# A two-layer conformer and attention trunk on one core: y gets its own buffer, layer 0's sum is transposed block by block unnormalised, ScalarE seeds the taps

## The reference

```python
# layer 0
a, b, z = split(rmsnorm(x, a_norm) @ a_w_in)             # 2048 x 6144
c  = causal_depthwise_conv(a * sigmoid(b), width 31) + conv_b
y  = silu(layernorm(c) * ln_g + ln_b) * silu(z)
x1 = x + y @ a_w_out                                     # 2048 x 2048
# layer 1
kv = rmsnorm(x1, kv_norm) @ w_kv                         # k, v of 3 groups, 16 heads of 128
q, z2 = split(rmsnorm(x1, b_norm) @ b_w_in)              # q of 3 groups, and a gate
o  = merged softmax attention of the 3 dilation groups, bias by distance
x2 = x1 + (o * silu(z2)) @ b_w_out
out = rmsnorm(x2, final_norm)
```

## Time and profile before

| | us |
|---|---|
| median of 3 runs | 1511.68 (1511.62 to 1514.68) |
| the profiled execution | 1510.1 |
| its span | 1508.3 |
| PE busy | 1462.2 |
| DVE busy | 793.9 |
| ACT busy | 689.1 |
| GpSimd busy | 386.7 |

### The profile page before, as it was taken

How to read it: one execution, slowest core, us unless ns; L and a number is a source line. 1 busy time by engine, 2 the same in 40 slices (tenths; PEclk the granted TensorE clock), 3 DMA queues, 4 the chain that set the end, 5 groups by cost and what they waited for, 6 DMA issues and landing times.

```text
span 1508.3 us, 28300 instructions
## 1 busy us (share of the span) xinstructions
PE 1462.2 (97%) x11478; PEld 1414.1 (94%) x11478; DVE 793.9 (53%) x1190; ACT 689.1 (46%) x989; POOL 386.7 (26%) x168
## 2 busy tenths in 40 slices
PE   6999998979999999999999999999999999999997
PEld 5999998868799999999999999999999999999886
DVE  3899999480274454544444444445454454444332
ACT  5434343464474444444444444444444444444543
POOL 4888887568600000000000000000000000000595
PEclk9999999989999999999999999999999999999999
DMA  9666666345399666656666666665665666653652
GB/s 256 176 193 184 183 195 182 117 134 184 111 275 238 179 176 173 183 161 188 187 170 178 167 179 179 178 186 156 191 178 167 177 176 176 184 159 115 251 195 84
DMA packets 454141, 268.52 MB, mean 178 GB/s; under 512 B 4353, under 2 KB 436481, under 8 KB 453426
## 3 DMA queue, kind: packets, MB, share of 16 engines
q1 hardware_dynamic: 454098, 267.99, 62.1%
q10 hardware_dynamic: 6, 0.02, 0.0%
HBM read 263.71 MB, written 4.29 MB: 178 GB/s over the span
## 4 chain that ended last, share of the span: by engine, by line
issue 76%; POOL 18%; PE 5%; POOLq 0%; DVE 0%; ACT 0%
POOL w_lo L271 18%; PE bank L307 2%; PE bank L308 2%; PE bank L309 2%; POOLq L270 0%; ACT bank L681 0%; DVE y L965 0%; DVE resid L949 0%; PE bank L1109 0%; ACT y L702 0%; PE bank L327 0%; PE bank L326 0%; PE bank L325 0%; PE bank L1111 0%; ACT stat L697 0%
## 5 line engine op out<-in xcount | busy, mean ns | idle before, releaser
L262 ACT ACTIVATE w_hi<-raw 128x1024 fp32r<-128x1024 f32 x480 | 506.6, 1059 | 471.5 <-PE bank L289 386.7
L271 POOL TENSOR_TENSOR w_lo<-raw,w_hi 128x1024 fp32r<-128x1024 f32 x160 | 385.7, 2416 | 1105.1 <-ACT w_hi L262 1105.0
L287 PE MATMUL bank<-act_a,w_hi 128*128 128x256 f32 x2304 | 651.0, 283 | 4.7 <-DVE act_b L869 2.4
L288 PE MATMUL bank<-act_a,w_hi 128*128 128x256 f32 x2304 | 646.4, 281 | 0.0
L289 PE MATMUL bank<-act_a,w_lo 128*128 128x256 f32 x2304 | 643.0, 279 | 0.0
L271 DVE TENSOR_TENSOR w_lo<-raw,w_hi 128x1024 fp32r<-128x1024 f32 x320 | 391.6, 1229 | 476.4 <-ACT w_hi L262 476.4
L287 PEld LDWEIGHTS bank<-act_a,w_hi 128*128 128x128 f32 x2304 | 434.6, 189 | 7.0 <-DVE act_b L869 2.6
L288 PEld LDWEIGHTS bank<-act_a,w_hi 128*128 128x128 f32 x2304 | 438.0, 190 | 0.1
L289 PEld LDWEIGHTS bank<-act_a,w_lo 128*128 128x128 f32 x2304 | 434.7, 189 | 0.0
L287 PE MATMUL bank<-act_b,w_hi 128*128 128x256 f32 x1024 | 288.1, 281 | 0.0
L288 PE MATMUL bank<-act_b,w_hi 128*128 128x256 f32 x1024 | 286.4, 280 | 0.0
(11 more groups left out here) (119 smaller groups left out, 767.2 us busy)
## 6 DMA issues: line engine op xcount, KB each, us to landing
raw<-w_kv_dram SPq DMA_DIRECT2D x96, 1024.0 KB, 6.0
raw<-b_w_in_dram SPq DMA_DIRECT2D x64, 1024.0 KB, 6.6
raw<-a_w_in_dram SPq DMA_DIRECT2D x48, 1024.0 KB, 5.9
raw<-a_w_out_dram SPq DMA_DIRECT2D x16, 1024.0 KB, 5.0
raw<-b_w_out_dram SPq DMA_DIRECT2D x16, 1024.0 KB, 5.1
bias<-bias_dram SPq DMA_DIRECT2D x16, 384.0 KB, 8.1
x_sb<-x_dram SPq DMA_DIRECT2D x2, 1024.0 KB, 7.4
resid_dram<-x_sb SPq DMA_DIRECT2D x1, 2048.0 KB, 7.9
```

The lines of the kernel that those rows point to most:

```text
L262: nc.scalar.activation(w_hi[:, stream.half_slot(half), :], raw[:, slot, part:part + HALF], ACT.Copy).then_inc(hi_done, 1)
L271: eng.tensor_tensor(w_lo[:, stream.half_slot(half), :], raw[:, slot, part:part + HALF], w_hi[:, stream.half_slot(half), :].bitcast(F32), A ...
L287: nc.tensor.matmul(dst[:, 0:S], wide_hi, source[:, kt, 0, :], start=(kt == 0), stop=False)
L288: nc.tensor.matmul(dst[:, 0:S], wide_hi, source[:, kt, 1, :], start=False, stop=False)
```

## The change

- `tap`, `seed_taps`: for channel blocks 2 to 15, ACT writes the two accumulators of taps 0 and 1. They lie in three banks in turn. 28 taps stand between two glus.
- The mean moves to z slab 7, the squares to slab 10, the variance to 10, the root to 12.
- y: swish goes from `conv` to three places in PSUM (`y_stage`), is gated there, and its parts go to `mem_y`, a buffer of its own that shares no memory with what z's products read. Swish and parts are one loop; weight slabs 0, 1, 2 of A_OUT are split at its steps 4, 11, 14.
- A block of x1 is transposed unnormalised during the next block (`turn_x1`), and ACT and DVE make the parts for layer 1 from it (`input_hi`, `input_lo`). Behind A_OUT stands only the last block's; PE goes on with QKV halves 0, a part of 1, and 2 around it.
- 1/rms enters behind the products: rows made by PE from scaled identities (`diag`, `anti`) multiply k and z (`scale_head`, DVE), the scores take it with their scale (`q_scale`), v takes it when its rows are copied (`v_scale`; four copies instead of two). ACT copies v and q only.
- SP stores x1 once it is added. ACT's AB loop is written out. Operand buffers have other addresses: all high parts together, then all low parts.

```diff
-Y_LOOP_SPLITS = {7: (2, (0,)), 14: (2, (1,))}
-LATE_Q_INPUT = {2: range(4, 8), 3: range(8, 12), 4: range(12, KT)}
+RAW_SLOTS, HALF_SLOTS = 5, 5
 U_RING = 4
-PAIR_TAPS = 26
-MEAN_SLAB, SQUARE_SLOT, VAR_SLAB, STD_SLOT = 8, 12, 11, 14
+PAIR_TAPS = 28
+SEEDED_FROM = 2
+ACC_BANKS = (4, 5, 7)
+MEAN_SLAB, SQUARE_SLOT, VAR_SLAB, STD_SLOT = 7, 10, 10, 12
+SPREAD = 8
+Y_LOOP_SLABS = (4, 11, 14)
+PART = KT * S
...
+        def act_a(kt, part):
+            first = part * (PART + SPREAD) + kt * S
+            return mem_a[:, first:first + S]
...
+        def y_in(kt, part):
+            first = part * PART + kt * S
+            return mem_y[:, first:first + S]
+        def y2_in(kt, part):
+            first = 80 + part * PART + kt * S
+            return mem_a[:, first:first + S]
...
+        y_stage = [bank[n][:, 0:S] for n in ACC_BANKS]
...
             for half in (2 * j, 2 * j + 1):
+                project_tiles(pe, stream, turn, half, range(KT // 2), dst, source, source_ready).then_inc(mm_done, 1)
...
+                    nc.tensor.matmul(dst[:, 0:S], wide_hi, source(kt, 1), start=False, stop=False)
+                    mm = nc.tensor.matmul(dst[:, 0:S], wide_lo, source(kt, 0),
...
                 mm.then_inc(mm_done, 1)
+        def turned(kt):
+            return bank[4 + 2 * (kt // RKT % 2) + kt % RKT // 2][:, (kt % 2) * S:(kt % 2 + 1) * S]
+        def acc_of(c, k):
...
-                    sp.wait_ge(x1_turned, TT * KT)
+                    sp.wait_ge(x1_added, TT * CHUNKS)
                     sp.dma_start(resid_dram.ap(), x_sb[:, :, :]).then_inc(resid_stored, 16)
...
+            def seed_taps(c):
+                act.wait_ge(u_ready, c + 1)
+                positive(act, tap_done, taps_before(c - 2))
+                for k in range(2):
+                    acc, tap = acc_of(c, k), param[:, c, k:k + 1]
+                    src = u[:, c % U_RING, k:k + S]
+                    if k == 0:
+                        nc.scalar.activation(acc, src, ACT.Identity, bias=param[:, c, ROW_CONV_B:ROW_CONV_B + 1],
+                                             scale=tap).then_inc(seeded, 1)
+                    else:
+                        nc.scalar.activation(acc, src, ACT.Copy, scale=tap).then_inc(seeded, 1)
+            for n in range(2, 2 * KT):
+                split_hi(act, AB, n // 4, n % 4)
+                if n >= 4 and n % 2 == 0:
+                    c = n // 2 - 2
+                    gate_b(c // 2, c % 2)
+                if n >= 5 + 2 * SEEDED_FROM and n % 2 == 1:
+                    seed_taps((n - 5) // 2)
...
+                if n in (1, 3):
+                    seed_taps(KT - 2 + n // 2)
...
+            for kt in range(KT + 1):
+                if kt < KT:
+                    act.wait_ge(ln_scaled, kt // 4 + 1)
+                    if kt >= 3:
+                        act.wait_ge(y_lo, kt - 2)
+                    nc.scalar.activation(y_stage[kt % 3], conv[:, kt, :], ACT.Silu,
+                                         bias=param[:, kt, ROW_LN_B:ROW_LN_B + 1],
+                                         scale=param[:, kt, ROW_LN_G:ROW_LN_G + 1]).then_inc(swished, 1)
+                if kt > 0:
+                    act.wait_ge(y_ready, kt)
+                    nc.scalar.activation(y_in(kt - 1, 0), y_stage[(kt - 1) % 3], ACT.Copy).then_inc(y_hi, 1)
+                if kt in Y_LOOP_SLABS:
+                    j = Y_LOOP_SLABS.index(kt)
+                    split_hi(act, A_OUT, 0, j)
+                    gate_z(KT - 3 + j)
...
+            def input_hi(c):
+                act.wait_ge(x1_turned, c + 1)
+                for kt in range(RKT * c, RKT * (c + 1)):
+                    nc.scalar.activation(act_a(kt, 0)[:, ::-1], turned(kt), ACT.Copy,
+                                         scale=param[:, kt, ROW_KV_NORM:ROW_KV_NORM + 1]).then_inc(kv_hi, 1)
+                for kt in range(RKT * c, RKT * (c + 1)):
+                    act.wait_ge(kv_lo, 2 * (kt // 2 + 1))
+                    nc.scalar.activation(act_b(kt, 0), turned(kt), ACT.Copy,
+                                         scale=param[:, kt, ROW_B_NORM:ROW_B_NORM + 1]).then_inc(qb_hi, 1)
...
+                if q == 3 and c > 0:
+                    input_hi(c - 1)
             split_hi(act, QKV, 0, 0)
+            split_hi(act, QKV, 0, 1, halves=(0,))
             for t in range(TT):
                 square_rows(CHUNKS - 1, t)
...
+            for t in range(TT):
                 act.wait_ge(x1_summed, t + 1)
                 nc.scalar.activation(std[:, t:t + 1], sq_sum[:, t:t + 1], ACT.Sqrt, bias=eps,
                                      scale=1.0 / D).then_inc(x1_std, 1)
...
             split_hi(act, QKV, 0, 1, halves=(1,))
+            act.wait_ge(v_scale_ready, 1)
...
+                    turned_v = bank[5 + b][:, 0:n * S].rearrange("p (g t d) -> p g t d", g=n, t=TT)
+                    for t in range(TT):
+                        nc.scalar.activation(v_rows[:, g0:g0 + n, t, :], turned_v[:, :, t, :], ACT.Copy,
+                                             scale=v_scale[:, t:t + 1]).then_inc(v_copied, 1)
...
+                before = taps_before(c) + (k if c < SEEDED_FROM else k - 2)
+                if c < SEEDED_FROM and k == 0:
                     dve.wait_ge(u_ready, c + 1)
-                    if c > 0:
-                        dve.wait_ge(tap_done, c * (TAPS + 1))
-                if k >= 2:
-                    dve.wait_ge(tap_done, c * (TAPS + 1) + (k - 1))
+                if c >= SEEDED_FROM:
+                    if k < 2:
+                        return
+                    if k == 2:
+                        dve.wait_ge(seeded, 2 * (c - SEEDED_FROM + 1))
+                if k >= (2 if c < SEEDED_FROM else 4):
+                    dve.wait_ge(tap_done, before - 1)
                 if k == 0:
...
+            for kt in range(KT + 1):
+                if kt < KT:
+                    dve.wait_ge(swished, kt + 1)
+                    dve.wait_ge(gate_ready, kt + 1)
+                    nc.vector.tensor_tensor(y_stage[kt % 3], y_stage[kt % 3], gate[:, kt, :],
+                                            ALU.mult).then_inc(y_ready, 1)
+                if kt > 0:
+                    dve.wait_ge(y_hi, kt)
+                    nc.vector.tensor_tensor(y_in(kt - 1, 1), y_stage[(kt - 1) % 3], y_in(kt - 1, 0).bitcast(F32),
+                                            ALU.subtract).then_inc(y_lo, 1)
...
+            def input_lo(c):
+                for kt in range(RKT * c, RKT * (c + 1)):
+                    dve.wait_ge(kv_hi, 2 * (kt // 2 + 1))
+                    nc.vector.scalar_tensor_tensor(
+                        out=act_a(kt, 1)[:, ::-1], in0=turned(kt), scalar=param[:, kt, ROW_KV_NORM:ROW_KV_NORM + 1],
+                        in1=act_a(kt, 0)[:, ::-1].bitcast(F32), op0=ALU.mult, op1=ALU.subtract).then_inc(kv_lo, 1)
+                for kt in range(RKT * c, RKT * (c + 1)):
+                    dve.wait_ge(qb_hi, 2 * (kt // 2 + 1))
+                    nc.vector.scalar_tensor_tensor(
+                        out=act_b(kt, 1), in0=turned(kt), scalar=param[:, kt, ROW_B_NORM:ROW_B_NORM + 1],
+                        in1=act_b(kt, 0).bitcast(F32), op0=ALU.mult, op1=ALU.subtract).then_inc(qb_lo, 1)
             for c in range(CHUNKS - 1):
                 for t in range(TT):
                     add_layer0(c, t)
+                if c > 0:
+                    input_lo(c - 1)
+            input_lo(CHUNKS - 2)
             split_lo(dve, QKV, 0, 0, lo_dve)
-            add_layer0(CHUNKS - 1, 0)
...
             split_lo(dve, QKV, 0, 1, lo_dve, halves=(0,))
...
+            for t in range(TT):
+                add_layer0(CHUNKS - 1, t)
+            for t in range(TT):
+                sum_squares(t, x1_squared, x1_summed)
+            input_lo(CHUNKS - 1)
+            for t in range(TT):
+                dve.wait_ge(x1_std, t + 1)
+                nc.vector.reciprocal(rstd[:, t:t + 1], std[:, t:t + 1]).then_inc(x1_rstd, 1)
+            dve.wait_ge(x1_rstd, TT)
+            for t in range(TT):
+                nc.vector.tensor_scalar(diag[:, t, :], ident[:, :], rstd[:, t:t + 1], None,
+                                        ALU.mult).then_inc(diag_ready, 1)
+                nc.vector.tensor_scalar(anti[:, t, ::-1], ident[:, :], rstd[:, t:t + 1], None,
+                                        ALU.mult).then_inc(diag_ready, 1)
+            nc.vector.tensor_scalar(q_scale, rstd, SCALE, None, ALU.mult).then_inc(r_rows_copied, 1)
             split_lo(dve, QKV, 0, 1, lo_dve, halves=(1,))
+            dve.wait_ge(r_rows_made, 1)
+            nc.vector.tensor_scalar(r_row[:, :], bank[2][:, 0:S], float(D), None, ALU.mult).then_inc(r_rows_copied, 1)
+            nc.vector.tensor_scalar(rk_row[:, ::-1], bank[2][:, 0:S], float(D), None,
+                                    ALU.mult).then_inc(r_rows_copied, 1)
+            dve.wait_ge(r_rows_made, 2)
+            nc.vector.tensor_scalar(v_scale, bank[3][:, 0:TT], float(D), None, ALU.mult).then_inc(v_scale_ready, 1)
```

(89 more changed lines are left out.)

177 lines of the change are left out of this document (59 added, 118 removed).

## The result

The changed kernel takes 1524.49 us (median of 4 runs, 1522.99 to 1525.56); the kernel before took 1512.87 beside it. Ratio 1.0075, interval 1.0058 to 1.0093: 11.6 us slower where no change was forecast.

What follows compares the result with a forecast made beforehand. TensorE, busy 97% of the span, was taken as the bound. Terms 2.6 − 8.0 − 3.4 − 9.7 + 3.0 + 18.8 − 3.7 + 0.8 − 0.3 summed to +0.1 us, forecasting 1511.8 us, range 1501 to 1518.

Steps and rivals of the forecast that it cites:

- New addresses of the operands: All matmuls: pace unchanged by the new operand addresses, 0; a 0.1% change of pace would be ±1.3 us.
- blocks 1 to 3: Output projection A after its first block: transposes moved inside, +3.0 us, and waits at two block ends, +18.8.
- E to the fifth half: From the end of output projection A to QKV's fifth half-slab: −3.7 us, and +0.8 for lost clock.
- Taps seeded: Conv loop: ScalarE seeds taps 0 and 1; PE waits 3.7 us against 1.1 before, +2.6 (bounds 0, +6).
- Mean, variance, handover of y: z stage into output projection: no wait at mean, −8.0 us, or variance, −3.4; y's own buffer, −9.7.
- The forecast wait of 0.7: First output block: PE waits 0.7 us for the second weight slab, split near 305.1.
- T1 and T2: Ends of output projection A's second and third blocks: crossed ScalarE and DVE queues, 2 × 9.4 = +18.8 us.
- Start of QKV: From output projection A's end to QKV's fifth half: store leaves earlier, −3.7 us (bounds −5 and −1).
- E': End of output projection A in the changed kernel, from which the QKV start times are counted.
- Heads: Attention heads: bank reads pass from ACT to DVE, covered, 0; +7 us if the cover were gone.
- the prediction's rivals: T1/T2 waits absent, 1493 us, 15% (half hidden, 1502, 5%); conv loop behind, 1521, 13%; heads lose cover, 1519, 7%.
- The one that reached furthest up, 1521: Conv loop falls behind at the GLU product of channels 7, 11 and 15, costing clock: 1521 us, 13%.

Runs made afterwards that it cites:

- e1: Kernel before, with only act_a and act_b at the addresses the change gives them: 1529.45 us, ratio 1.0124.
- e2: Changed kernel with the operand address layout of the kernel before, y and y2 staying contiguous: 1506.29 us, ratio 0.9964.
- e5: Changed kernel with both input_lo ahead of add_layer0 and the padded operand addresses of the kernel before: 1485.12 us, ratio 0.9832.
- e3: Changed kernel with input_lo(c - 1) moved ahead of add_layer0(c, t) in VectorE's queue: 1503.26 us, ratio 0.9959.
- e4: Changed kernel with every operand tile, high or low, at a multiple of 512 bytes: 1532.88 us, one run.
- e10: Changed kernel with moved input_lo, buffer a all at 224 bytes past a multiple of 512, buffer b all at 160: 1498.42 us, one run.
- e9: Changed kernel with moved input_lo, both buffers' tiles all 192 bytes past a multiple of 512: 1479.99 us, ratio 0.9786.
- e11: Changed kernel with moved input_lo, buffer a all at 96 bytes past a multiple of 512, buffer b all at 208: 1510.59 us, one run.
- e6: Changed kernel with moved input_lo, buffer a all at 192 bytes past a multiple of 512, buffer b all at 256: 1493.06 us, one run.
- e7: Changed kernel with moved input_lo, buffer a all at 128 bytes past a multiple of 512, buffer b high parts at 0, low at 256: 1511.08 us, one run.
- e8: Changed kernel with moved input_lo and another offset layout for each of buffers a and b: 1494.77 us, one run.

## Why the prediction was wrong, point by point

The step that failed is the sentence *"New addresses of the operands: the matmul pace is the same for act_a, act_b and w_hi now, so 0; a 0.1% change of pace would be ±1.3"*. It was priced at 0, and measures +20.6 for the moving operands (e1, e2 show it alone) and −4.7 for y. The inference was faulty: act_a and act_b had the same pace because both had the same layout, and the change gave them another. w_hi, the moving operand of the output projections, lies at multiples of 512, and its half took the same 2.80 us only beside a y in the padded layout: beside the moved y it takes 2.72. Equal paces in the layouts of one trace say nothing about others. The bound of 0.1% had no row behind it.

Stage by stage, in the profiled executions; "pace" is tiles × 6.2 ns, or −6.1 ns for each of the 768 matmuls of 512 columns (227 ns instead of 233: y, their stationary operand, moved too, to multiples of 512; no run moves y alone):

| stage | forecast | measured | of it pace | the rest |
|---|---|---|---|---|
| AB loop | +3.7 | +7.1 | +3.2 | 3.0 clock, 0.9 |
| z, mean, variance, wait for y | −20.9 | −19.3 | +1.6 | −20.9 |
| first output block | −1.3 | −2.5 | −0.6 | −1.9 |
| blocks 1 to 3 | +21.8 | +20.6 | −1.8 | +22.4 |
| E to the fifth half | −2.9 | −4.0 | +0.2 | −4.2 |
| heads, to the last projection | 0 | +15.3 | +15.7 | −0.4 |
| last projection, end; start | −0.3 | −2.0 | −2.3 | +0.3 |

(The conv loop's +2.6 is split in this table: four new waits of 3.7 in the AB loop, and the 1.1 of before, which lie in z's stage.) The forecast sums to +0.1, the measured column to +15.2.

*Taps seeded.* Right in mechanism, and hidden. DVE waits 2.6 us for its first seed (2.0 forecast), in the rows of DVE after:

```profile
L812 DVE SCALAR_TENSOR_TENSOR bank<-u,param,bank 128x256 f32<-128x256 f32 x448 | 179.4, 481 | 2.6 <-ACT bank L567 2.6
...
L839 DVE TENSOR_TENSOR u<-bank,b_sig x16: 408/415/425, 47.4 to 222.7; 128x256 f32<-128x256 f32 x16
```

The last product starts at 222.7 instead of 217.2, but PE had slowed down as much: DVE's lag was paid by the pace. Where the pace is the old one (e2, e5), three PE idles of about 1 us stand at 104, 150 and 207 us, where the forecast had four, of 0.9, 1.4, 0.3 and 1.2.

*Mean, variance, handover of y.* Right, to 0.1 us once the pace is taken off. The forecast wait of 0.7 in the first output block did not come. That is not because PE arrives there 5 us later than forecast: in e5 PE starts the block at 302.1 (302.2 forecast), and it takes 21.78 us without a wait. The term was mis-sized: ScalarE splits the second slab at 303.4, not at 305.1, as this line of e5's timeline shows:

```profile
303.36 2.06 ACT L291 ACTIVATE w_hi<-raw 128x1024 fp32r<-128x1024 f32 x2
```


*T1 and T2.* Right in place, mechanism and size: PE starts at T1 + 7.67 (forecast 7.4), and the halves behind lose 5.26 and 4.56 less the undisturbed 12 × 0.227 = 2.72, so 2.5 and 1.8 (2.0 each). e3 takes both away: 19.7 us in these blocks, 18.8 forecast.

*Start of QKV.* The timeline of SP, then ACT, after, against the earlier trace rows:

```profile
417.46 0.34 SPq L450 DMA_DIRECT2D resid_dram<-x_sb  x1
...
425.56 1.05 ACT L293 ACTIVATE w_hi<-raw 128x1024 fp32r<-128x1024 f32 x1
430.47 3.91 ACT L293 ACTIVATE w_hi<-raw 128x1024 fp32r<-128x1024 f32 x4 [3.85 <-DVE stat L939]
```

The store goes out 0.9 after E' (1.0 forecast), ACT waits for v_scale until E' + 13.9 (14.1), the fifth half starts at E' + 17.8 (18.1). PE's idle before half 3 is 2.64 (2.7). Behind it the granted clock is 0.71 over 5.87 us, thus 0.29 × 5.87 = 1.7 us lost where 0.8 was charged. It costs nothing, for the fifth half waits for its splits in any case: e3 keeps the full clock there and takes the same 17.9 us from E' to the fifth half (17.8 after), with 1.9 us of waiting for the first k copy instead of 0.4. The idle and what follows it, in e3:

```profile
403.60:406.24 2.64, 0.27 (x3) 1.00 1.16 310
406.24:412.13 5.89, 4.01 (x33) 1.00 1.19 292
```

The Trainium skill, "TensorE: Matmul & The Clock Gate", section "Part 4: PE-mode transpose", says that transposes do not count as activity; the prediction drew from it that this idle, behind 9.3 us of nearly only real matmuls at 1.00, would be free of a clock loss. The traces go both ways: behind this idle the clock stayed at 1.00 up to the fifth half in e2, e3, e4 and e10, and fell to 0.50 for a while in after, e5 to e9 and e11. So the idle is not safely free, and what decides is not the work ahead of it, since after and e3 share that (81 matmuls in 9.32 us at 1.00). What part the transposes have no run here shows.
The Trainium skill, "TensorE: Matmul & The Clock Gate", section "Back-to-back issue gap", gives N/2.4 + 2.5 ns for an isolated matmul of N columns, an estimate of 109 ns at 256, and says nothing of addresses. Here, before and after, the pace is 115.4 to 122.1 ns at full clock and changes with the addresses, and even the fastest stretches (e9, 113.3) stay above the estimate: the measurements decide.

*Heads.* No new wait, as forecast; all of the 15.3 is pace.

*The start.* 3.0 of the 15.2 are the stretch at 1.2 GHz from 31.98. From 29 to 32 us, ahead of it, PE starts only 3 or 4 matmuls a us, but so it does in e3, where the clock stays at 1.00. e4, e6, e7 and e9 have such a stretch in the same place, the others not. What brings it about stays open; with it taken off, 12.2 are left against 11.6 in the medians.

None of the prediction's rivals came true. The one that reached furthest up, 1521, had the wrong mechanism, and the range ended at 1518, for the pace had been given ±1.3.

## What to carry to other kernels

When a change moves or re-lays an operand that PE reads thousands of times, its addresses are an edit with a price of their own: compare the matmuls started in a stretch where PE never rests, and if only one layout is in the trace, give the unknown a wide bound rather than 0. When two in-order queues feed each other, look for the pair of steps that each wait behind the other's later work; here moving one call ahead of another was worth 19 to 21 us. Repair such costs one by one and check that they add: here they did, and only then could it be seen that the change without these two costs is worth 27 us (e5), y's pace included. And before a pace is called a property of a layout, look whether it is the same in every stretch and in a second run: at offset 192 it was not.

## What the runs showed of the hardware

- The pace of fp32r matmuls of 128x128 by 256 columns depends on the byte offset of the moving operand: 120.0 ns at 0 past a multiple of 512 (e4), 117.8 at 64 (e8), and up to 122.1 for the low part at 224 between high parts at 192 (after, e1, e3).
- At 192 there are two paces, 113.3 and 117.8 ns, which hold over long stretches (e6, e9). The same code at the same addresses had the one in e9 and the other in e6 from 60 to 100 us.
- The layout of the stationary operand seems to count too: 512 columns against a y at multiples of 512 take 227 ns (after, e2 to e11), against a y in the padded layout 233 (before), and 233 with its parts at 192 and 224 (e1). No run moves y alone, but the last projection, whose own code is otherwise the same, shows the same step.
- In the kernel before the pace repeats with period four in the tile's number (the low matmul 117.0, 115.4, 120.5, 116.3): its stride of 2112 bytes steps the offset by 64 each time, so four tiles make 256 bytes, and 0 and 256 have nearly the same pace (120.0, 119.8).
- An idle of 2.64 us behind 9.32 us of unbroken work at 1.00 was followed by 5.87 us at a granted 0.71 in after, and by 5.89 us at 1.00 in e3; idles of 7.67 were followed by 0.50 and 0.59 (after).
- The 16 subtractions that make y's low parts took 410 to 2627 ns, median 411, with both operands in SBUF (before), and 412 to 424 with one of them in PSUM (after). What made some of them long no run shows.
